# Another order for the late mixer stages of a two-layer hybrid trunk with experts

## The reference

```python
def hybrid_layer(x, ...):
    h = rms_norm(x, norm_mix)
    proj = jnp.einsum('btd,dp->btp', h, w_in).astype(jnp.float32)
    (g_qkv, g_z, g_b, g_a, r_q, r_k, r_v, r_g,
     m_qk, m_v, m_o, m_i, m_f) = jnp.split(proj, np.cumsum(IN_SPLITS)[:-1].tolist(), axis=-1)
    y_gdn = gdn_mixer(g_qkv, g_z, g_b, g_a, gdn_conv, gdn_a_log, gdn_dt_bias, gdn_norm)
    y_ret = retention_mixer(r_q, r_k, r_v, r_g, ret_norm)
    y_mlstm = mlstm_mixer(m_qk, m_v, m_o, m_i, m_f, mlstm_conv, mlstm_i_bias, mlstm_f_bias, mlstm_norm)
    mix = jnp.concatenate([y_gdn, y_ret, y_mlstm], axis=-1).astype(x.dtype)
    x = x + jnp.einsum('btm,md->btd', mix, w_out)
    x = x + hierarchical_moe(rms_norm(x, norm_ffn), router_group, router_expert, router_bias,
                             expert_gate, expert_up, expert_down)
    return x
```

## Time and profile before

| | |
|---|---|
| median of three timed runs | 917.0 us (916.55 to 917.73) |
| the profiled execution: time | 918.45 us |
| its span | 916.7 us |
| busy in the span: PE, weight loads, DVE, ACT | 823.6, 585.9, 298.6, 201.1 us |
| granted TensorE clock, mean | 0.966 of 2.4 GHz |
| moved by DMA | 249.03 MB, mean 272 GB/s |

### The profile page before, as it was taken

How to read it: one execution, slowest core, us unless ns; L and a number is a source line. 1 busy time by engine, 2 the same in 40 slices (tenths; PEclk the granted TensorE clock), 3 DMA queues, 4 the chain that set the end, 5 groups by cost and what they waited for, 6 DMA issues and landing times.

```text
span 916.7 us, 16751 instructions
## 1 busy us (share of the span) xinstructions
PE 823.6 (90%) x6664; PEld 585.9 (64%) x6664; DVE 298.6 (33%) x720; ACT 201.1 (22%) x425; POOL 2.2 (0%) x12
## 2 busy tenths in 40 slices
PE   6999799979999997799899998989799999999665
PEld 4877698757865654356578767877588555544322
DVE  1546331455351111111146452216453311211102
ACT  1251531341311000010113335332312110010002
POOL 0000000000000000000000000000000000000000
PEclk9999999979999998799999999999799999999999
DMA  9742163223689999999984231623167899999995
GB/s 354 317 152 92 47 234 134 94 92 138 253 343 421 420 421 420 419 422 421 419 336 161 66 119 59 229 82 138 46 234 305 326 420 420 421 421 420 421 421 208
DMA packets 35929, 249.03 MB, mean 272 GB/s; under 512 B 3984, under 2 KB 4496, under 8 KB 6800
## 3 DMA queue, kind: packets, MB, share of 16 engines
q1 hardware_dynamic: 35424, 247.30, 67.3%
q10 hardware_dynamic: 432, 0.71, 0.2%
HBM read 246.96 MB, written 1.05 MB: 271 GB/s over the span
## 4 chain that ended last, share of the span: by engine, by line
PE 65%; DMA 18%; DVE 7%; ACT 5%; issue 3%; SPq 1%; PEldq 1%; DVEq 0%; PEld 0%; ACTq 0%; POOLq 0%
PE ps L526 18%; DMA ring<-e_down 15%; PE ps L958 9%; PE ps L833 6%; PE ps L928 5%; PE ps L979 4%; PE ps L665 4%; DMA work<-e_down 3%; PE ps L991 2%; PE ps L987 2%; PE ps L706 2%; ACT work L1105 1%; PE ps L541 1%; PE ps L755 1%; PE ps L738 1%
## 5 line engine op out<-in xcount | busy, mean ns | idle before, releaser
L526 PE MATMUL ps<-hT,ring 128*128 128x256 f32 x864 | 192.7, 383 | 1.7 <-DVEq L1289 1.7
L526 PEld LDWEIGHTS ps<-hT,ring 128*128 128x128 f32 x864 | 163.9, 191 | 28.3 <-DVEq L1289 4.1
L958 PE MATMUL ps<-ring,hT 128*32 128x256 f32 x1408 | 84.4, 385 | 8.4 <-DMA ring<-e_gate 4.6
L928 PEld LDWEIGHTS ps<-work,xn 128*128 128x128 f32 x640 | 73.0, 192 | 9.7 <-issue 7.6
L928 PE MATMUL ps<-work,xn 128*128 128x128 f32 x640 | 76.8, 278 | 1.9 <-DVE work L1626 1.9
L958 PEld LDWEIGHTS ps<-ring,hT 128*32 128x32 f32 x1408 | 43.0, 111 | 45.8 <-issue 11.3
L833 PE MATMUL ps<-xn,ring 128*128 128x256 f32 x256 | 58.0, 382 | 0.0
L833 PEld LDWEIGHTS ps<-xn,ring 128*128 128x128 f32 x256 | 48.0, 190 | 7.5 <-issue 1.0
L1626 DVE TENSOR_TENSOR work<-shapes,sel 128x128 f32<-128x128 f32 x40 | 9.9, 288 | 127.5 <-PE ps L965 127.2
L1643 DVE TENSOR_TENSOR hT<-ps,pars 128x512 f32<-128x512 f32 x40 | 27.7, 692 | 48.6 <-PE ps L928 48.6
L979 PE MATMUL ps<-ring,work 128*32 128x512 f32 x272 | 33.0, 597 | 9.7 <-DMA ring<-e_down 6.3
(11 more groups left out here) (285 smaller groups left out, 908.8 us busy)
## 6 DMA issues: line engine op xcount, KB each, us to landing
ring<-e_gate SPq DMA_DIRECT2D x44, 1024.0 KB, 26.3
ring<-e_up SPq DMA_DIRECT2D x36, 1024.0 KB, 15.2
ring<-w_mix SPq DMA_DIRECT2D x34, 1024.0 KB, 5.3
ring<-e_down SPq DMA_DIRECT2D x28, 1024.0 KB, 27.3
work<-e_down SPq DMA_DIRECT2D x24, 1024.0 KB, 19.8
work<-e_gate SPq DMA_DIRECT2D x12, 1024.0 KB, 9.9
work<-e_up SPq DMA_DIRECT2D x12, 1024.0 KB, 28.1
more_buf<-e_down SPq DMA_DIRECT2D x8, 1024.0 KB, 17.6
```

The costliest lines, as they stand in the source:

```text
L526: mm = pe.matmul(bank[:, ct * T:(ct + 1) * T], w[:, k, ct * P:(ct + 1) * P], hT3[:, k, :], start=(k == 0), stop=(k == KD - 1))
L928: mm = pe.matmul(ps[:, 4 + 3 * half_, kk * P:(kk + 1) * P], xn3[:, j, k * P:(k + 1) * P], Psel[:, j, :], start=(j == 0), stop=(j == TT - 1))
L958: mm = pe.matmul(ps[32 * e:32 * e + 32, 5 + m, 0:DE], hq[:, k, 32 * e:32 * e + 32], w[:, c0:c0 + DE], start=(k == 0), stop=(k == KD - 1), ...
```

## The change

It puts the late mixer's work into another order on PE, ACT and DVE, deals out the PSUM banks for it by hand, and moves buffers. The load order of the experts' slots S3 and S1 is exchanged.

```diff
 def expert_slots(ring):
-    return ["N0", "N1"] + ring[0:8] + ["S0", "S3", "K2", "S1", "S2", "K"] + ring[8:12] + ["L", "X"]
+    return ["N0", "N1"] + ring[0:8] + ["S0", "S1", "K2", "S3", "S2", "K"] + ring[8:12] + ["L", "X"]
 def psum_plan():
-    after = [("rqk", 0), "u1", "t1", ("rqk", 1), "u2"] + [("o", p) for p in range(GP)] + [("on", p) for p in range(GP)]
...
-    banks += [(i + 0) % 8 for i in range(len(after))]
...
+    late = [(("rqk", 0), 0), ("u1", 1), (("rqk", 1), 2), ("t1", 3), (("rsw", 0), 4), ("u2", 5), (("rsw", 1), 6), (("mdec", 0), 7)]
+    late += [(("o", p), p) for p in range(GP)] + [(("mdec", 1), 3), (("mdec", 2), 4)] + [(("on", p), 5 + p) for p in range(GP)]
+    late += [(("mqk", 0), 3), (("rs", 0), 0), (("rs", 1), 1), (("rs", 2), 2), (("rs", 3), 5), (("mqk", 1), 4), (("o", 3), 6), (("o", 4), 7)]
+    late += [(("em", p), p) for p in range(MP)] + [(("on", 3), 5), (("on", 4), 3), (("mqk", 2), 4)]
+    late += [(("wo", 0), 0), (("ms", 0), 6), (("ms", 1), 7), (("ms", 2), 5), (("ms", 3), 4), (("wo", 1), 1), (("ms", 4), 2), (("ms", 5), 3)]
+    late += [(("o", 5), 6), (("o", 6), 7), (("o", 7), 5), (("wo", 2), 2), (("on", 5), 4), (("wo", 3), 3), (("on", 6), 6), (("on", 7), 7)]
...
-        rkf = kq[:, 1280:1792].rearrange("p (c t) -> p c t", c=RP)
+        rkf = work[:, NKQ:NKQ + 512].rearrange("p (c t) -> p c t", c=RP)
-        mprob = raw[:, 0:MH * 384].rearrange("p (h t) -> p h t", h=MH)
-        rraw = kq[:, 2560:3584].rearrange("p (a c t) -> p a c t", a=2, c=2)
-        rtmp = kq[:, 3584:4096].rearrange("p (c t) -> p c t", c=2)
+        mprob = xxt[:, 0:MH * 384].rearrange("p (h t) -> p h t", h=MH)
+        rraw = [kf[:, 0:2, :], raw[:, 1792:2304].rearrange("p (c t) -> p c t", c=2)]
+        rtmp = kqp[:, 0:RP, 1, :]
-        rrr = rraw[:, 0, :, :]
+        rrr = kq[:, 2560:3072].rearrange("p (c t) -> p c t", c=2)
-        mem = [late_buf[:, 1280:1536], hT3[:, 6, :], hT3[:, 7, :]]
+        mem = [late_buf[:, 1280 + T * p:1280 + T * (p + 1)] for p in range(MP)]
```

On PE, behind `u1`:

```diff
                 done(mm, "u1")
+                project_cm(("rqk", 1))
                 bank = begin("t1")
...
-                project_cm(("rqk", 1))
+                swap_halves(0)
                 bank = begin("u2")
...
+                swap_halves(1)
                 m_decay(0)
+                pe.wait_ge(u_ready, upto(l, u_ready, 2))
+                for p in range(GP):
+                    bank = begin(("o", p))
+                    done(pair_out(bank, 0, head(vb, p), [KQ[:, 2 * p, 1, :], KQ[:, 2 * p + 1, 1, :]]), ("o", p))
+                m_decay(1)
+                m_decay(2)
+                for p in range(GP):
+                    head_norm(p, raw3[:, p, :])
+                project_cm(("mqk", 0))
+                pe.wait_ge(rq_ready, upto(l, rq_ready, 2))
+                for h in range(RH):
+                    r_scores(h)
+                project_cm(("mqk", 1))
+                pe.wait_ge(val_ready, upto(l, val_ready, 1))
                 for p in range(RP):
                     bank = begin(("o", 3 + p))
                     pe.wait_ge(p_ready, upto(l, p_ready, 2 * p + 2))
                     done(pair_out(bank, 0, head(vr, p), rprob[2 * p:2 * p + 2]), ("o", 3 + p))
-                release()
+                for p in range(MP):
+                    m_floors(p)
                 for p in range(RP):
                     head_norm(3 + p, rsq[:, p, :])
...
+                project_cm(("mqk", 2))
...
+                pe.wait_ge(mix_ready, upto(l, mix_ready, GP + RP))
+                begin_out(0)
+                release()
+                for p in range(2):
+                    pe.wait_ge(mq_ready, upto(l, mq_ready, 4 + p))
+                    m_scores(p)
+                begin_out(1)
+                pe.wait_ge(mq_ready, upto(l, mq_ready, 6))
+                m_scores(2)
                 pe.wait_ge(val_ready, upto(l, val_ready, 4))
                 m_out(0)
...
                 buffers_read(("ms", 5), 3)
                 m_out(1)
+                m_out(2)
                 begin_out(2)
+                buffers_read(("o", 7), 3)
                 head_norm(5, msq[:, 0, :])
-                m_out(2)
                 begin_out(3)
-                buffers_read(("o", 7), 3)
                 head_norm(6, msq[:, 1, :])
+                head_norm(7, msq[:, 2, :])
                 pe.wait_ge(mix_ready, upto(l, mix_ready, 6))
```

```diff
                 m_weights(0)
-                act.wait_ge(rq_ready, upto(l, rq_ready, 2))
+                act.wait_ge(conv_m_go, upto(l, conv_m_go, 1))
+                mlstm_in(0)
+                m_weights(1)
+                m_weights(2)
+                mlstm_in(1)
                 for p in range(RP):
                     bank = get(("o", 3 + p))
                     act.activation(rsq[:, p, :], bank[:, 0:T], ACT.Square).then_inc(o_sq_ready, 1)
+                for p in range(MP):
+                    m_floor(p)
                 for p in range(RP):
                     out_rr(3 + p, rrr[:, p, :])
...
+                for t in range(4):
+                    mlstm_silu(t)
+                mlstm_in(2)
+                for t in (4, 5):
+                    mlstm_silu(t)
+                act.preload_act_table_set(LN_EXP)
                 m_abs(0)
+                m_abs(1)
                 m_square(0)
...
```

More of the change, by code:

```diff
@@ L158, in psum_plan @@
     banks += [(i + 2) % 6 for i in range(len(inv))] + [6 + i % 2 for i in range(len(beside))]
-    after = [("rqk", 0), "u1", "t1", ("rqk", 1), "u2"] + [("o", p) for p in range(GP)] + [("on", p) for p in range(GP)]
[L160 to L163, removed]
-    banks += [(i + 0) % 8 for i in range(len(after))]
[L166 to L170, removed]
+    late = [(("rqk", 0), 0), ("u1", 1), (("rqk", 1), 2), ("t1", 3), (("rsw", 0), 4), ("u2", 5), (("rsw", 1), 6), (("mdec", 0), 7)]
[4 more added lines that the diff above has]
+    late += [(("o", 5), 6), (("o", 6), 7), (("o", 7), 5), (("wo", 2), 2), (("on", 5), 4), (("wo", 3), 3), (("on", 6), 6), (("on", 7), 7)]
+    late += [(("xt", 0), 4), (("xt", 2), 6), (("xt", 1), 5), (("xt", 3), 7), ("logits", 0), ("rank", 5)]
+    return list(zip(order, banks)) + late
 def trunk(nc, x_in, consts, level_masks, params, w_mix, router_w, e_gate, e_up, e_down, gain_final, out):
@@ L726, in _, with swap_halves @@
                 done(mm, "t1")
-                project_cm(("rqk", 1))
+                def swap_halves(a):
+                    bank = begin(("rsw", a))
+                    pe.wait_ge(rraw_ready, upto(l, rraw_ready, a + 1))
+                    done(pe.matmul(bank[:, :], c("swap"), rraw[a], start=True, stop=True), ("rsw", a))
+                swap_halves(0)
                 bank = begin("u2")
@@ L745, in head @@
                     return lambda a, j: of[:, j, (2 * p + a) * HD:(2 * p + a + 1) * HD]
[L747 to L750, removed]
                 def head_norm(cidx, src):
@@ L755, in head_norm, with r_scores @@
                     done(pe.matmul(bank[:, 0:T], c("headsum"), src, start=True, stop=True), ("on", cidx))
[L757 to L768, removed]
+                def r_scores(h):
                     bank = begin(("rs", h))
@@ L865, in _ @@
                     project_out(n, [5])
-                head_norm(7, msq[:, 2, :])
                 pe.wait_ge(mix_ready, upto(l, mix_ready, 7))
@@ L1138, in _, with swapped @@
                 act.preload_act_table_set(LN_EXP)
+                def swapped(a):
+                    bank = get(("rqk", a))
+                    link(act.activation(rraw[a], bank.rearrange("p (c t) -> p c t", c=2), ACT.Copy))
+                    act.sem_inc(rraw_ready, 1)
+                    act.sem_inc(free[bank_of[("rqk", a)][0]], 1)
                 for i, name in enumerate(("u1", "u2")):
+                    swapped(i)
                     bank = get(name)
@@ L1153, in _ @@
                     act.activation(raw3[:, p, :], bank[:, 0:T], ACT.Square).then_inc(o_sq_ready, 1)
-                for a in range(2):
-                    bank = get(("rqk", a))
-                    link(act.activation(rraw[:, a, :, :], bank[:, :], ACT.Copy))
-                    act.sem_inc(rraw_ready, 1)
-                    act.sem_inc(free[bank_of[("rqk", a)][0]], 1)
                 for p in range(GP):
@@ new lines, in _ @@
+                for p in range(GP):
+                    bank = get(("o", p))
+                    head_result(p, bank[:, 0:T], raw3[:, 3 + p, :])
+                    free_(("o", p))
+                link(dve.memset(cin_m[:, :, 0:3], 0.0))
+                dve.sem_inc(conv_m_go, 1)
+                m_exponents(2)
+                for t in (0, 1):
+                    conv(9 + t, cin_m, acc_m, wm(t))
+                for h in range(RH):
+                    bank = get(("rs", h))
+                    dve.wait_ge(rdec_ready, upto(l, rdec_ready, h + 1))
+                    link(dve.scalar_tensor_tensor(out=rprob[h], in0=bank[:, 0:384], scalar=QK_SCALE, in1=rprob[h],
```

(5 more changed lines are left out.)

117 lines of the change are left out of this document (36 added, 81 removed).

## The result

The changed kernel takes 885.8 us, median of 4 runs (884.51 to 887.22), against 916.77 (915.82 to 917.73) of the kernel before on the same chip: ratio 0.9659 [0.9641, 0.9676], 31.0 us less. I had forecast 891 in a range from 887 to 901.

The account below looks back on a forecast made before the run. The expert load stream's start, set by PE's late mixer, was taken to bound each layer. Removed idle less new idle plus clock gave 12.5 and 13.6 us, together 26.1 off the time before, so 891 us, range 887 to 901.

Parts of the forecast that it names:

- What bounds the kernel: Layer's end is the expert load stream's start plus fixed bytes; PE time saved in the late mixer passes through.
- (1) Removed idle: Late mixer, PE: the new order covers today's waits, 9.72 us in layer 0 and 9.48 in layer 1.
- (2) new idle: Late mixer, PE: new waits of 1.3 us per layer, including 0.8 at mqk 0 and 0.2 for the unseen.
- (3) Clock: Late mixer, PE: busy time lost to half clock comes back, 4.1 us in layer 0 and 5.4 in layer 1.
- Rival A: Late mixer: the clock falls anyway, costing 4 us per layer, so 899 us; chance 0.12.
- B: Late mixer: DVE or ACT is late at a tight place, 3 us per layer, so 897 us; chance 0.12.
- C: Expert loads: a mid slot is late and the stream starts no earlier than 263.4, so 910 to 917 us; chance 0.03.
- D: Late mixer: the clock falls in small matmuls behind rqk 1 and stays down through projections, so 928 us; chance 0.03.
- (4) Loads at nothing: Load queue on SP: later release of mid slots costs nothing, covered by 8 us between 223 and 231.5.
- no arithmetic is added or removed: the same matmuls: Late mixer: same matmuls, DVE and ACT instructions of the same sizes; only order, banks, places and mid slot loads change.
- the sum: Both late mixers: removed idle less new idle plus clock, 12.5 us in layer 0 and 13.6 in layer 1, together 26.1.
- My walk by starts: Late mixer: step-by-step timing that adds starts, not busy times; 14 us gained per layer, 888 to 889 us.

Follow-up runs that it names:

- scores-first run: The changed kernel with mLSTM scores 0 and 1 ahead of output projection 0 instead of behind it; 895.44 us, ratio 0.9764.
- with fillers: The kernel before with nine filler matmuls in the long wait for retention products, two ahead of o 4, five ahead of norm 3; 914.78 us, ratio 0.9969.
- reference run: The changed kernel with one more POOL register instruction per expert quarter, holding the extra rounds at zero or above; 888.81 us, ratio 0.9693.

## Why the prediction was wrong, and what of it was right

**What bounds the kernel**: right. The end of a layer is the start of the load stream plus a length that hardly changes, 189.25 us before and 189.24 after in layer 0, and 190.33 and 189.12 in layer 1; and where the loads ahead of it were late by a slot, this length grew by a slot. Two readings were loose: the second dip of PEclk in the late mixers is in slice 29 and not 28, with slice 17, in an expert stage, as deep as either; and between the four ring loads and the 263.43 two more loads go out, into `late_buf` and `xT`.

**(1) Removed idle and (2) new idle**: right in place. L741 does not wait for the products (forecast 184.6 against 184.7; measured 183.33 against 183.78). mqk 0 waits 0.66 for 0.8, the transposes 0.3 as before, and the 0.2 that I had added for the unseen was not needed: 0.96 and 0.94 us in place of 1.3, which gives 0.34 and 0.36 more.

**(3) Clock**: right in size, some 3.8 and 5.0 for 4.1 and 5.4, and PEclk is 1.00 in both late mixers. I had called my figures the upper end of what PE's busy time could give back, and it gave back 6.4 and 7.6. Rival A (0.12) did not come, nor did B, whose tight places all held, nor C and D; but the scores-first run shows the clock falling, behind two waits of 2.05 us together among the scores.

**(4) Loads at nothing**: right. Middle slots at 206.03 and 210.48 (forecast 208 and 215), ring loads at 227.93 (231.5), the first block's landing at 436.43 (440): each ahead of the forecast, the later two by the surplus of the stretch and the 1.1 us ahead of it.

**The step that failed** is "no arithmetic is added or removed: the same matmuls", as I used it in the sum. I took PE's busy time as fixed but for the clock; so the sum lacks a term. The same matmuls take some 91.15 us at full clock in the old order and 88.56 in the new: 2.6 per layer, 5.2 in both, more than the 4.9 by which the sum was short. By the runs, 7 breaks fewer at 0.15 and one pair no longer parted at 0.68 make 1.7 of it; at the 0.25 that the break of mqk 0 cost they would make 2.4. The rest, 0.2 to 0.9 per layer, stays open. One candidate can be read and was not tested: the old order also goes from one kind of group to another more often, and the four records of one floor take 0.58 us up to the next start by themselves (layer 1 with fillers, at 653.08) and 0.47 where three floors stand together (12 in 1.40, at 185.13). With the 2.6 and the idle the layers come to 8.76 + 3.8 + 2.6 = 15.2 and 8.54 + 5.0 + 2.6 = 16.1, against 15.14 and 16.17; as the 2.6 is what the clock leaves of the busy time, this shows how the gain divides and is no test of it.

My walk by starts, which may hold some of this, had given 14 us for a layer, and I used it only for the low end. The remaining 2.3 us of the two spans lie outside what the change touches:

- ahead of rqk 0 of layer 0, 1.1 us, where the clock fell once in both kernels, at 103 to 109 before and at 94 to 98 after;
- in layer 1's expert stage, from the first used slot's load to the last landing, 1.2 us;
- between these parts, 0.3 won from the last landing of layer 0 to rqk 0 of layer 1, and 0.4 lost from layer 1's transposes to its first used slot's load.

I had allowed nothing for them. They differ from kernel to kernel where the code is the same, as the reference run shows, and why they do is open.

## What to carry to other kernels

Where loads end a stage, look for what starts their stream: PE time ahead of that start passes through in full, and slots may be released late only as long as the queue of loads has slack. A list of an engine's waits also prices what it does not show: each break between groups of matmuls cost 0.15 us of busy time in one run here and 0.25 in another, and a wait between the matmuls of two heads of 64 rows 0.75 in all. When a new order is priced, let two sums, busy times and starts, agree before one of them is trusted; and once the order stands, look at which bank each remaining wait is for, as two changes of bank numbers took away waits of 0.66 and 0.86 us per layer here.

## What the runs showed of the hardware

- Two heads of 64 rows take 0.80 us back to back and 0.75 more when a wait parts them.
- The granted clock fell to 0.5 behind waits of 0.26 and 1.79 us among small matmuls (scores first) and behind 1.34 and 0.37 (layer 0 with fillers), and in the kernel before, layer 1 near 657, behind 0.76 and 0.36. It stayed at 1.00 behind 1.30 and 0.36 (layer 1 with fillers), the same place as the last two, and in the kernel before over 160.00 to 168.20 with PE busy 6.49 of 8.20 us. The Trainium skill, TensorE: Matmul & The Clock Gate, in A second HAM failure mode, says of another kernel, in bf16, that short and frequent idling between groups makes the clock swing. The fall near 657 agrees with that; the changed kernel, which cycles through all eight banks at 1.00, does not.
- In the early mixer, where PE's code is the same, the clock fell at 94 to 98 us in the changed kernel, at 103 to 109 in the kernel before, and at both places in the reference run, whose span is 3.2 us longer than the changed kernel's with the same stretch of 89.52 us.
